# Folded projections in the first layer, another order for the first norm, and adaLN slabs moved by a table

## Chip, core and metric

One core of one Trainium2 chip runs the whole program once per call. The metric is the device time in microseconds (us) of that execution. Five instruction queues work side by side: TensorE (matmuls; PE in the rows, its weight loads PEld), VectorE (DVE), ScalarE (ACT), GpSimd (POOL) and SyncE (SP, which here only issues DMAs). Each queue runs its instructions in the order in which they were written; semaphores are the only coupling.

## What is computed

A batch of one sequence of 256 tokens and 1024 channels goes through three layers in float32. Layer 1 is a mixer (attention with a forget gate, beside a short convolution) and a SwiGLU network; layers 2 and 3 are attention (block-wise, then differential) and a SwiGLU network each, modulated by a vector `c`. Cut to what the change touches:

```python
def first_block(x, ...):
    h = rmsnorm(x, norm_mix_pre)
    proj = h @ w_in          # q, k, v, f_logit, g_b, g_c, hc, gate_conv, gate_attn
    ya = g_b * causal_depthwise_conv(g_c * hc, conv_w)
    yb = forgetting_attention(q, k, v, log_sigmoid(f_logit + b_f))
    merged = sigmoid(gate_conv) * (ya @ w_branch[0]) + sigmoid(gate_attn) * (yb @ w_branch[1])
    x = x + rmsnorm(merged @ w_out, norm_mix_post)
    return x + rmsnorm(swiglu(rmsnorm(x, norm_ffn_pre)), norm_ffn_post)

def second_block(x, c, ...):                  # twice
    mod = silu(c) @ ada_w[i] + ada_b[i]       # shift, scale, gain of two norms
    h = rms_norm(x, g0) * (1 + sc_a) + sh_a
    x = x + g_a * rms_norm(attention_i(h), g1)
    h = rms_norm(x, g2) * (1 + sc_f) + sh_f
    x = x + g_f * rms_norm(swiglu(h), g3)
```

## The kernel before

**Tiles.** The tokens are two tiles t of 128; a channel block k is 128 channels, so x is 2 x 8 blocks. Every weight comes as a slab of 128 x 2048 float32 (1 MB). 159 main slabs (`MAIN`: `v1` 0 and 1, `qk1` 2 to 5, `mix` 6 to 19, `branch` 20 to 23, `out1` 24 to 27, the first network from 28 on) and 48 `ada` slabs, which hold the rows of `ada_w`, form one stream. SyncE loads stream item i into `raw[i % 8]` (L500) once item i - 8 has left its place: a main slab when TensorE has used it, an `ada` slab when VectorE has summed it.

**Precision.** Each product is made of three TensorE products in a rounded format. ScalarE rounds a slab to `high` (L506, `act_round`), VectorE subtracts to `low` (L512, `dve_rest`, written over `raw`); activations are split the same way into `h_hi` and `h_lo`. `act_next` and `dve_next` round the slab three ahead of the one in work and, on VectorE, first sum the `ada` slabs that stand before it in the stream (L521, two reductions of 128 x 1024 for each slab). `load_order` holds the table `plan` that says behind which main slabs the `ada` slabs come.

**Two forms of a projection.** `pe_still` (L585 to L587) keeps weight blocks still and sends 256 tokens past: for each of 16 weight blocks high x hi, high x lo, low x hi, 48 matmuls of 256 columns into one PSUM bank. `pe_both` (L623, L628) sends hi and lo side by side: 16 matmuls of 512 columns for high, then 16 of 256 columns for low, into two banks; ScalarE copies the lo half out (`act_low`, L635) and VectorE adds the hi half (`dve_low`, L643 or L645; signal `joined`). Before, `pe_still` is used for the four `qk1`, for `mix` 0 to 5 and for gates 6 and 7 (12 slabs); everything later that could be folded is.

**Start.** x tile 0, x tile 1, slab 0 in two halves are loaded in this order. The sums of squares go half to ScalarE (L352), half to VectorE (L1486); GpSimd makes the power (L364); x is scaled (L369; of tile 1 the left half by GpSimd, L1686, the right half by ScalarE); TensorE transposes it (L320, `pe_turn`); ScalarE applies the column gain from PSUM into `work` (L332, `act_affine`); VectorE casts to `h_hi` (L346) and subtracts to `h_lo` (L348). `pe_first_values` starts the values product; the second `v1` slab follows in `pe_moving` (L668 to L670), and the gate logits are copied by VectorE (L1512) before TensorE adds them up (L1213).

**First norm behind a layer.** `branch` ends in `merged` (VectorE L1603, L1608, ScalarE L1409, VectorE L1611), `out1` is the wide product, and its post norm (`dve_post_norm`: L420, L358, L435, then L369) gives the scaled x that TensorE transposes in the middle of `out1`'s last products. On GpSimd, `pool_gain` stores a gain column (L486) and loads it as rows (L490).

## Time and profile before

| | us |
|---|---|
| median of 3 runs (lowest, highest) | 963.48 (962.64, 963.85) |
| profiled execution, its own time | 962.54 |
| its span, first to last instruction | 961.2 |
| TensorE busy | 953.2 |
| VectorE busy | 740.0 |
| ScalarE busy | 544.8 |

The span lies 1.3 us under the profiled execution's own time, and that execution 0.94 us under the median. Matmul ends are modelled and overlap, so the pitch of matmuls is read from start to start, and waits from the idle time in brackets behind a row.

### The profile page before, as it was taken

Reading aid. Unit: us, or ns where it says so; the run is one execution under the profiler, and the core shown is the slowest. Engines: PE = TensorE matmul, PEld = TensorE weight load, DVE = VectorE, ACT = ScalarE, POOL = GpSimd, SP = SyncE. Lnnn points to the kernel's source line nnn. Section 1 sums busy time; section 2 is a strip of 40 time slices with the busy share of each in tenths; the row PEclk is TensorE's granted clock in tenths of the full one; section 3 lists DMA queues with packets and bytes.
Section 4 is the critical chain, followed back from the end, with each engine's and each line's share of the span. In section 5 each row is a group of like instructions: output and inputs, shape, how many; then the busy total and the mean of one; then the engine's idle time right before and its main releaser. Section 6 shows DMA issues by size and latency. Waiting matters only on the chain.

```text
span 961.2 us, 13438 instructions
## 1 busy us (share of the span) xinstructions
PE 953.2 (99%) x5418; PEld 827.7 (86%) x5418; DVE 740.0 (77%) x1145; ACT 544.8 (57%) x838; POOL 34.2 (4%) x58
## 2 busy tenths in 40 slices
PE   9999999999999999999999999999999999999997
PEld 7999989888888888888888888888888888888886
DVE  7799978788877767988678878766897678766563
ACT  6745553565455656665565454656776675454551
POOL 2000000020000001000000000001000100000000
PEclk9999999999999999999999999999999999999999
DMA  9877788498777753776467677763743266668511
GB/s 366 335 276 263 262 308 313 173 200 343 269 295 300 286 204 135 270 269 264 185 248 296 247 293 271 270 250 137 241 138 125 88 243 239 219 184 320 176 44 45
DMA packets 33151, 225.64 MB, mean 235 GB/s; under 512 B 4058, under 2 KB 4341, under 8 KB 6720
## 3 DMA queue, kind: packets, MB, share of 16 engines
q1 hardware_dynamic: 30960, 219.43, 61.8%
q0 software_dynamic: 1696, 5.08, 2.0%
q8 instruction: 43, 0.70, 0.3%
q10 hardware_dynamic: 432, 0.26, 0.1%
q14 instruction: 20, 0.16, 0.0%
HBM read 223.49 MB, written 1.26 MB: 234 GB/s over the span
## 4 chain that ended last, share of the span: by engine, by line
PE 93%; DVE 2%; DMA 2%; ACT 2%; SPq 0%; POOL 0%; issue 0%; DVEq 0%
PE psum L623 30%; PE psum L628 16%; PE psum L668 10%; PE psum L669 10%; PE psum L670 10%; PE psum L585 3%; PE psum L586 3%; PE psum L587 3%; DMA raw<-in_qk 2%; PE psum L888 2%; PE psum L740 1%; PE psum L739 1%; PE psum L741 1%; PE psum L320 1%; PE psum L956 1%; PE psum L601 0%
## 5 line engine op out<-in xcount | busy, mean ns | idle before, releaser
L512 DVE TENSOR_TENSOR low<-raw,high 128x2048 fp32r<-128x2048 f32 (+1 forms) x160 | 361.1, 2275 | 95.1 <-ACT high L506 95.0
L506 ACT ACTIVATE high<-raw 128x2048 fp32r<-128x2048 f32 (+1 forms) x160 | 299.9, 1897 | 15.1 <-DMA raw<-in_moba_qk 4.8
L623 PE MATMUL psum<-h_both,high 128*128 128x512 f32 x1272 | 305.3, 392 | 0.0
L623 PEld LDWEIGHTS psum<-h_both,high 128*128 128x128 f32 x1272 | 235.5, 188 | 48.2 <-issue 1.5
L628 PEld LDWEIGHTS psum<-h_both,low 128*128 128x128 f32 x1312 | 168.3, 191 | 6.4
L628 PE MATMUL psum<-h_both,low 128*128 128x256 f32 x1312 | 170.2, 283 | 0.0
L668 PE MATMUL psum<-high,y_hi 128*128 128x512 f32 x328 | 129.3, 394 | 0.0
L669 PE MATMUL psum<-low,y_hi 128*128 128x512 f32 x328 | 128.1, 391 | 0.0
L670 PE MATMUL psum<-high,y_lo 128*128 128x512 f32 x328 | 127.8, 390 | 0.0
L635 ACT ACTIVATE work_v<-psum 128x256 f32<-128x256 f32 x120 | 45.6, 383 | 142.2 <-PE psum L628 142.2
L521 DVE CUSTOM_DVE_ANT_0 raw<-raw,c_row 128x1024 f32<-128x1024 f32 x96 | 113.4, 1219 | 0.0
L670 PEld LDWEIGHTS psum<-high,y_lo 128*128 128x128 f32 x328 | 61.6, 188 | 13.1
L668 PEld LDWEIGHTS psum<-high,y_hi 128*128 128x128 f32 x328 | 61.7, 188 | 11.9 <-DVE y_lo L978 0.2
L669 PEld LDWEIGHTS psum<-low,y_hi 128*128 128x128 f32 x328 | 61.8, 188 | 11.4
L643 DVE TENSOR_TENSOR work_v<-psum,work_v 128x256 f32<-128x256 f32 x120 | 47.9, 420 | 23.4 <-ACT work_v L635 23.3
L585 PE MATMUL psum<-h_both,high 128*128 128x256 f32 x192 | 55.3, 288 | 0.0
L586 PE MATMUL psum<-h_both,high 128*128 128x256 f32 x192 | 54.4, 283 | 0.0
L587 PE MATMUL psum<-h_both,low 128*128 128x256 f32 x192 | 54.4, 283 | 0.0
L809 ACT ACTIVATE y_hi<-work_v 128x512 fp32r<-128x512 f32 x30 | 19.0, 632 | 48.4 <-DVE work_v L831 48.4
L668 PE MATMUL psum<-high,h_both 128*128 128x512 f32 x104 | 41.6, 400 | 0.1
L670 PE MATMUL psum<-high,h_both 128*128 128x512 f32 x104 | 40.6, 391 | 0.0
L669 PE MATMUL psum<-low,h_both 128*128 128x512 f32 x104 | 40.6, 390 | 0.0
(195 smaller groups left out, 1033.6 us busy)
## 6 DMA issues: line engine op xcount, KB each, us to landing
raw<-in_gate_up SPq DMA_DIRECT2D x66, 1024.0 KB, 5.5
raw<-in_ada SPq DMA_DIRECT2D x48, 1024.0 KB, 4.9
raw<-in_down SPq DMA_DIRECT2D x33, 1024.0 KB, 4.9
raw<-in_mix SPq DMA_DIRECT2D x14, 1024.0 KB, 6.9
raw<-in_moba_qk SPq DMA_DIRECT2D x8, 1024.0 KB, 5.2
raw<-in_diff_qk SPq DMA_DIRECT2D x8, 1024.0 KB, 4.9
raw<-in_qk SPq DMA_DIRECT2D x4, 1024.0 KB, 16.2
raw<-in_branch SPq DMA_DIRECT2D x4, 1024.0 KB, 6.3
```

Source lines behind the costliest of these rows:

```text
L506: nc.scalar.activation(high[n % N_HI][:, s], raw[i % N_RAW][:, s], ACT.Copy).then_inc(*rounded.up(n if key is None else key))
L512: nc.vector.tensor_tensor(low[i % N_RAW][:, s], raw[i % N_RAW][:, s], high[n % N_HI][:, s].bitcast(F32), ALU.subtract).then_inc(*rest.up(key))
L521: last = nc.vector.tensor_tensor_reduce(out=w, in0=w, in1=c_row[:, :], scale=1.0, scalar=0.0, op0=ALU.mult, op1=ALU.add, accum_out=mod_raw ...
L585: nc.tensor.matmul(to, a, hi(k), start=first, stop=False)
L586: nc.tensor.matmul(to, a, lo(k), start=False, stop=False)
L587: m = nc.tensor.matmul(to, r, hi(k), start=False, stop=last and j > j0)
L623: nc.tensor.matmul(o[:, :], a, h_both[:, k, :, :], start=k == 0, stop=False)
L628: m = nc.tensor.matmul(o[:, 0:S], wl[:, k, j * P:(j + 1) * P], h_hi[:, k, :], start=False, stop=k == KC - 1)
L643: m = nc.vector.tensor_tensor(place[:, j, :], o, place[:, j, :], ALU.add)
L668: nc.tensor.matmul(psum[b][:, :], hi(k0 + k, t), vh, start=first, stop=False)
L669: nc.tensor.matmul(psum[b][:, :], hi(k0 + k, t), vl, start=False, stop=False)
L670: m = nc.tensor.matmul(psum[b][:, :], lo(k0 + k, t), vh, start=False, stop=last)
```

## The change

1. Twelve first-layer slabs go from `pe_still` to `pe_both`, with bank numbers fixed for some; `act_low` and `dve_low` take their results out, and the products that used to read PSUM now read the joined tile.
2. The first norm: `act_affine` writes `h_hi` itself, and `h_lo` is made block by block from PSUM with one `scalar_tensor_tensor`; tile 1 is scaled half by VectorE and half by ScalarE; slab 0's first half is loaded and rounded ahead of x's second tile; slab 1 is rounded in halves, and TensorE may begin on the first half; three filling matmuls go.
3. `plan`: 14, 11, 8, 11, 4 `ada` slabs in five stretches become 9, 14, 8, 13, 4. Before, 14 stood behind main slabs 4, 5, 6, 8, 9, 10, 12, 13, 15, 16, 17, 19, 20, 22; now 9 stand behind 9, 11, 13, 15, 18, 20, 22, 24, 27.
4. GpSimd waits for the scaled x of tile 1 before it stores a gain column (three places).

```diff
-    plan = [(14, 4, 22), (11, nets[0][0] + 4, nets[0][0] + 24), (8, nets[0][1] + 4, nets[1][0] - 2),
-            (11, nets[1][0] + 3, nets[1][0] + 26), (4, nets[2][0] + 4, nets[2][0] + 16)]
+    plan = [(9, 9, 27), (14, nets[0][0] + 2, nets[0][0] + 24), (8, nets[0][1] + 4, nets[1][0] - 2),
+            (13, nets[1][0] + 2, nets[1][0] + 25), (4, nets[2][0] + 4, nets[2][0] + 16)]
...
         def act_affine(stage, t, g):
-                o, to = psum[bank_of[stage, t, g]][:, (k - a) * P:(k - a + 1) * P], work_b[:, k, tile_of(t)]
+                o = psum[bank_of[stage, t, g]][:, (k - a) * P:(k - a + 1) * P]
+                to = (h_hi if stage == "in" else work_b)[:, k, tile_of(t)]
...
         def dve_split_h(stage, t, a, b):
+            if stage == "in":
+                ...
+                yield from dve.wait_ge(affined, (stage, t, k1 - 1))
+                for k in range(a, b):
+                    m = nc.vector.scalar_tensor_tensor(
+                        out=h_lo[:, k, w], in0=psum[bank_of[stage, t, g]][:, (k - k0) * P:(k - k0 + 1) * P], scalar=scale[:, k:k + 1],
+                        in1=h_hi[:, k, w].bitcast(F32), op0=ALU.mult, op1=ALU.subtract)
...
             def qk(g, keys):
-                yield from pe_still("qk1", 2 * keys + g, h_of, ready, [[(produced, ("k1", g)) if keys else (evacuated, ("q1", g))]])
+                yield from pe_both("qk1", 2 * keys + g, ready, at=(6, 7) if keys == 1 and g == 0 else (5, 6) if keys else (None, None))
...
-                yield from pe_still("mix", g, h_of, ready, [[(produced, ("conv", g))]])
+                yield from pe_both("mix", g, ready, at=(None, None) if g else (4, 6))
...
                 yield from dve_next("mix", 4 + g)
-                yield from dve.wait_ge(slab, ("mix", 4 + g))
-                yield from dve.wait_ge(evacuated, ("zc", g))
-                nc.vector.tensor_tensor(zc[:, two, :], pair(bank_of["mix", 4 + g, 0]), zc[:, two, :], ALU.mult).then_inc(
-                    *produced.up(("z", g)))
+                yield from dve_low(("mix", 4 + g), ya[:, two, :])
+                yield from dve.wait_ge(joined, ("mix", 4 + g, 1))
+                nc.vector.tensor_tensor(zc[:, two, :], ya[:, two, :], zc[:, two, :], ALU.mult).then_inc(*produced.up(("z", g)))
...
             yield from pool_post_norm(1)
+            yield from pool.wait_ge(scaled, (1, NT - 1, 1))
             yield from pool_gain(0, 1, 0)
...
         def sync():
-            for t in range(NT):
-                nc.sync.dma_start(x_res[:, t, :], dram["x"][tile_of(t), :]).then_inc(*x_in[t].up("rows", by=16))
             first, half = dram["v1"][0], SLAB // 2
+            nc.sync.dma_start(x_res[:, 0, :], dram["x"][tile_of(0), :]).then_inc(*x_in[0].up("rows", by=16))
             nc.sync.dma_start(raw[0][:, 0:half], first[:, 0:half]).then_inc(*raw_first.up("a", by=16))
+            nc.sync.dma_start(x_res[:, 1, :], dram["x"][tile_of(1), :]).then_inc(*x_in[1].up("rows", by=16))
             nc.sync.dma_start(raw[0][:, half:], first[:, half:]).then_inc(*raw_in[0].up(0, by=16))
```

The table of `ada` slabs moves instructions at places that the diff does not show. SyncE, the loads of the `out1` slabs (24 to 27), before:

```order
L500 DMA raw6<-in_out1 128x2048 [waits slab]
L500 DMA raw7<-in_out1 128x2048 [waits summed]
L500 DMA raw0<-in_out1 128x2048 [waits slab]
L500 DMA raw1<-in_out1 128x2048 [waits summed]
L500 DMA raw2<-in_gate_up1 128x2048 [waits slab]
```

and after, where `raw1` was held by slab 20, the first `branch` slab:

```order
L511 DMA raw7<-in_out1 128x2048 [waits summed]
L511 DMA raw0<-in_ada 128x2048 [waits slab]
L511 DMA raw1<-in_out1 128x2048 [waits slab]
L511 DMA raw2<-in_out1 128x2048 [waits summed]
L511 DMA raw3<-in_out1 128x2048 [waits slab]
L511 DMA raw4<-in_ada 128x2048 [waits slab]
```

Two `ada` slabs now stand among the `out1` slabs, and slab 25 waits for a slab that TensorE has used instead of one that VectorE has summed.

VectorE, between the first and the third `branch` slab (L1603 before and L1615 after are the products with the gates; `low6`, `low7` before are slabs 24 and 25), before:

```order
L1603 TENSOR_TENSOR work<-psum1,work 128x512 [waits slab]
L512 TENSOR_TENSOR low6<-raw6,high0 128x2048 [waits rounded]
L512 TENSOR_TENSOR low7<-raw7,high1 128x2048 [waits rounded]
L1603 TENSOR_TENSOR work<-psum2,work 128x512 [waits slab]
L1603 TENSOR_TENSOR work<-psum3,work 128x512 [waits slab]
L1603 TENSOR_TENSOR bias<-psum0,bias 128x512 [waits slab]
```

and after (`low7`, `low1` are slabs 24 and 25):

```order
L1615 TENSOR_TENSOR work<-psum1,work 128x512 [waits slab]
L523 TENSOR_TENSOR low7<-raw7,high0 128x2048 [waits rounded]
L532 ISA raw0,mod_raw<-raw0,c_row 128x1024 [waits raw_in0]
L532 ISA mod_raw 128x1
L532 ISA raw0,mod_raw<-raw0,c_row 128x1024
L532 ISA mod_raw 128x1
L486 SCALAR_TENSOR_TENSOR mod_raw<-mod_raw,mod_given 128x8 [waits summed]
L490 TENSOR_TENSOR mod_cols<-mod_raw,mod_given 128x8 [waits summed]
L523 TENSOR_TENSOR low1<-raw1,high1 128x2048 [waits rounded]
L1615 TENSOR_TENSOR work<-psum2,work 128x512 [waits slab]
L1615 TENSOR_TENSOR work<-psum3,work 128x512 [waits slab]
L1615 TENSOR_TENSOR bias<-psum0,bias 128x512 [waits slab]
```

A sum of an `ada` slab has come between slabs 24 and 25.

VectorE, ahead of the first post norm (L420 before, L431 after, is its first instruction), before:

```order
L1611 TENSOR_TENSOR h_both<-bias,h_both 128x2x256 [waits hi_made]
L512 TENSOR_TENSOR low1<-raw1,high3 128x2048 [waits rounded]
L512 TENSOR_TENSOR low2<-raw2,high4 128x2048 [waits rounded]
L512 TENSOR_TENSOR low3<-raw3,high5 128x2048 [waits rounded]
L420 TENSOR_TENSOR work<-psum4,gain0 128x512 [waits squared,gain_in0,produced]
```

and after:

```order
L1623 TENSOR_TENSOR h_both<-bias,h_both 128x2x256 [waits hi_made]
L523 TENSOR_TENSOR low3<-raw3,high3 128x2048 [waits rounded]
L532 ISA raw4,mod_raw<-raw4,c_row 128x1024 [waits raw_in4]
L532 ISA mod_raw 128x1
L532 ISA raw4,mod_raw<-raw4,c_row 128x1024
L532 ISA mod_raw 128x1
L523 TENSOR_TENSOR low5<-raw5,high4 128x2048 [waits rounded]
L523 TENSOR_TENSOR low6<-raw6,high5 128x2048 [waits rounded]
L431 TENSOR_TENSOR work<-psum4,gain0 128x512 [waits squared,gain_in0,produced]
```

One more sum stands among the three subtractions in front of the norm.

## Rows read from the trace of the kernel before

**Rows 1.** The page: parts 1 and 2, busy time and granted clock.

```profile
PE 953.2 (99%) x5418; PEld 827.7 (86%) x5418; DVE 740.0 (77%) x1145; ACT 544.8 (57%) x838; POOL 34.2 (4%) x58
PEclk9999999999999999999999999999999999999999
```

**Rows 2.** Waits of TensorE: who waited, for whom, us in all, times, longest.

```profile
PE psum L888 <- DVE ck L1552: 0.4, 1, 0.4
```

**Rows 3.** Timeline of TensorE (start us, us, line), then pieces of the chain.

```profile
26.21 0.28 PE L587 MATMUL psum<-h_both,low 128*128 128x256 f32 x1
...
31.96 0.28 PE L587 MATMUL psum<-h_both,low 128*128 128x256 f32 x1
```

```profile
119.06 1.91 PE psum L628 x16
120.97 3.65 PE psum L623 x16
```

**Rows 4.** Timeline of the first 25 us; last, VectorE's instructions grouped by shape.

```profile
4.87 0.63 ACT L352 ACTIVATE work_v<-x_res 128x512 f32<-128x512 f32 x1 [1.47 <-DMA x_res<-in_x]
...
6.30 0.63 ACT L352 ACTIVATE work_v<-x_res 128x512 f32<-128x512 f32 x1 [0.71 <-DMA x_res<-in_x]
...
16.86 6.70 DVE L512 TENSOR_TENSOR low<-raw,high 128x2048 fp32r<-128x2048 f32 x3 [0.25 <-ACT high L506]
...
19.21 0.19 PEld L668 LDWEIGHTS psum<-high,h_both 128*128 128x128 f32 x1 [0.66 <-DVE low L512]
...
23.47 0.67 DVE L1512 COPY work<-psum 16x512 f32<-16x512 f32 x1
...
24.89 0.38 PE L1213 MATMUL psum<-cols,work 16*128 16x8 f32 x2
...
L901 DVE SCALAR_TENSOR_TENSOR prob<-psum,c_q,const 128x128 f32<-128x128 f32 x8 | 2.8, 344 | 0.0
```

**Rows 5.** VectorE in the first layer: windows, two timeline rows, a group of the page.

```profile
34.00:100.00 66.00, 65.58 (x545) 62.93 (x544) 64.54 (x118) 34.25 (x59) 0.00 (x0) 1.00 0.73 271
...
38.32 1.22 DVE L521 CUSTOM_DVE_ANT_0 raw<-raw,c_row 128x1024 f32<-128x1024 f32 x1
...
44.13 0.86 DVE L1552 TENSOR_TENSOR ck<-psum,ck 8x256 fp32r<-8x256 f32 x2 [0.55 <-ACT ck L1364]
...
L643 DVE TENSOR_TENSOR work_v<-psum,work_v 128x256 f32<-128x256 f32 x120 | 47.9, 420 | 23.4 <-ACT work_v L635 23.3
```

The first row's columns are: stretch, its length, busy us of PE, PEld, DVE, ACT, POOL (instructions), granted clock, DMA share, GB/s.

**Rows 6.** Timeline of VectorE and GpSimd in the norms behind two networks.

```profile
378.62 1.19 DVE L369 TENSOR_SCALAR work<-x_res,stat 128x512 f32<-128x512 f32 x2 [0.66 <-POOL stat L364]
...
667.51 1.05 POOL L486 DMA_DIRECT2D gain_dram<-gain_col  x1
667.59 1.19 DVE L369 TENSOR_SCALAR work<-x_res,stat 128x512 f32<-128x512 f32 x2 [0.66 <-POOL stat L364]
```

**Rows 7.** Timeline from `branch` to the first post norm, four queues.

```profile
143.27 6.56 SPq L500 DMA_DIRECT2D raw<-in_out  x4
...
148.21 1.92 ACT L506 ACTIVATE high<-raw 128x2048 fp32r<-128x2048 f32 x1 [1.55 <-DMA raw<-in_out]
...
148.84 0.28 PE L585 MATMUL psum<-y_hi,high 128*128 128x256 f32 x1
...
152.61 2.29 DVE L512 TENSOR_TENSOR low<-raw,high 128x2048 fp32r<-128x2048 f32 x1 [0.16 <-ACT high L506]
...
157.68 0.69 DVE L1603 TENSOR_TENSOR bias<-psum,bias 128x512 f32<-128x512 f32 x1 [1.58 <-PE psum L587]
...
173.32 6.70 DVE L512 TENSOR_TENSOR low<-raw,high 128x2048 fp32r<-128x2048 f32 x3 [1.11 <-ACT high L506]
...
179.93 0.68 DVE L420 TENSOR_TENSOR work<-psum,gain 128x512 f32<-128x512 f32 x1
...
184.65 0.88 DVE L369 TENSOR_SCALAR work<-x_res,stat 128x512 f32<-128x512 f32 x2 [0.67 <-POOL stat L364]
...
185.28 1.06 PE L320 MATMUL psum<-const,work 128*128 128x128 f32 x8
```

More of the change, by code:

```diff
@@ L663, in pe_moving @@
                 for k in range(kcs):
+                    if n == 1 and k == kcs // 2:
+                        yield from pe.wait_ge(rest, n)
                     for signal, key in ready(k0 + k, t):
@@ L1171, in pe_first_values @@
                     nc.tensor.matmul(o[:, :], h_hi[:, k, tile_of(0)], wl[:, k, :], start=False, stop=False)
[L1172 to L1173 removed]
+                for k in ks:
+                    for signal, made in ready(k, 0):
+                        yield from pe.wait_ge(signal, made)
+                    nc.tensor.matmul(o[:, :], h_lo[:, k, tile_of(0)], wh[:, k, :], start=False, stop=False)
             o = yield from bank(("v1", 1, 0), *freed_by_values("v1")(1, 0), at=6)
```

134 lines of the change are left out of this document (68 added, 66 removed).

## Prediction

> **What bounds the kernel now.** I read the page's busy times first, then TensorE's waits, then the pitch of its matmuls, then the timelines of the places that the change touches. TensorE is busy 953.2 of 961.2 us, at a granted clock of 9 tenths or more in every slice [rows 1]; the only wait of it that the change aims at behind the start is one of 0.4 us, for `ck` from VectorE [rows 2]. So time can be saved in three ways only: fewer or cheaper matmuls, an earlier start, shorter waits; and anything that makes TensorE wait is paid in full. VectorE is the engine to watch. Between 34 and 100 us it is busy 64.5 of 66.0 [rows 5] and still makes TensorE wait hardly at all, because its work lies three slabs ahead. Where that lead ends, at the first post norm, the reader should look hardest: TensorE's transposes begin at 185.28, and the scaled x that they read comes from an instruction pair that begins at 184.65 [rows 7]; its first half ends some 0.5 later, so there is about 0.1 us to spare.
>
> **The folding.** A still slab is 48 matmuls: from 26.21 to 31.96, 48 starts on, is 5.75 us. A folded slab is 16 of 512 columns and 16 of 256: 3.65 + 1.91 = 5.56 [rows 3]. That is 0.19 a slab, for 12 slabs **-2.3** (-2.0 to -2.6, for first matmuls behind other work). What it adds lies on ScalarE (two copies, where there was one or none; it has idle time) and on VectorE: 24 additions of 256 columns from PSUM at 0.42 [rows 5], about 10 us. VectorE has no such room today, but the table takes 7 of 11 sums away that stood up to main slab 17; a sum is two reductions of 1.14 start to start (the row gives 1.22 with its tail), 2.3 together, so 16 us go. VectorE therefore gets lighter by some 6 us there.
>
> **The `ck` wait.** `ck` is ready once VectorE has worked off what is in front of it; the first tables' sums (two by then, 4.6 us) are gone and four additions (1.5) come. It should be ready near 43.1 in place of 45.0 [rows 5], while TensorE arrives about 1 us sooner than today. The wait goes: **-0.5** (0 to -0.6; the row says 0.4, start to start it is 0.58).
>
> **A new wait for banks.** Folded slabs take two banks, and these come free only when VectorE has added. The tight one is `mix` 0: its second bank is the second of `mix` 5, and only one pass of 16 matmuls and three transposes (2.2 us) lies between. In VectorE's queue, an `ada` sum (2.3), a subtraction (2.2) and two attention pieces stand ahead of that addition. Counted through its queue from `ck` on, I find it done some 0.3 late: **+0.3** (0 to +1.0).
>
> **The start.** x's second tile landed 1.43 us behind the first (4.87, 6.30); now half a slab of the same 512 KB goes between, so all that needs both tiles comes 1.4 later. The 16 new split instructions have a row like them: PSUM and SBUF in, 128 x 128, 0.344 each [rows 4], against pairs of a cast and a subtraction before. ScalarE's rounding of the first half fills the time that it waited. Followed through the four queues with these durations, VectorE comes to slab 1's subtraction at 17.0 (16.86 before) and to the copy of the logits at 23.7 (23.47). TensorE no longer waits 0.66 for all of slab 1, because a half is enough, is done with the values at 24.5, and starts the gate sums at about 24.6 in place of 24.89 [rows 4]: **-0.3** (-0.8 to +0.3). What is late next is VectorE's copy of the logits.
>
> **GpSimd's later stores.** In two norms the scaling pair takes 1.19, where it takes 0.88 elsewhere [rows 6, 7]; in one of them the store of the gain column, 1.05 long, begins 0.08 before it [rows 6]. TensorE stands waiting for that pair in both. Behind the new wait the store begins after it: twice 0.31, of which I take **-0.5** (0 to -0.6). Nothing on GpSimd behind the store is due for many us. The Trainium skill (SBUF — State Buffer, "Who interferes with whom") says that of VectorE in a two-port mode and GpSimd one blocks the other for a whole instruction. By that the stores could give back up to 1.05 each, 1.6 more than I take in all; the measured lengthening, 0.31, decides.
>
> **What the table adds.** Two `ada` slabs now stand among the `out1` slabs, and this is the costliest part.
> First, slab 25. Its load waits for the first `branch` slab, which TensorE leaves at 148.84; a load of this kind landed 4.94 after its issue (143.27 to 148.21), so it lands at 153.8. Rounding takes 1.92, to 155.7; the subtraction 2.2, to 158.0; two products with the gates 1.28, to 159.3. The third `branch` slab's product, which began at 157.68, is then 1.6 late. From there to 173.32 VectorE and ScalarE hand each other one step after the other, so the delay is not made up: the subtractions for `out1` begin at 174.9.
> Second, a sum of 2.3 us stands between them, in front of the norm. The norm's first instruction moves from 179.93 to 183.8, 3.9 later. I count no slack in the steps from there to the scaling, which follow on one another as before. So the scaled x is 3.9 late, and TensorE, with 0.1 to spare, stands for 3.8 [all rows 7]: **+3.8** (+2.2 if slab 25 lands in time, +4.0). TensorE has no other work to put there: what follows stands behind the transposes in its queue.
> The denser tables in the first two networks (14 for 11 and 13 for 11 sums) cost VectorE 7 and 5 us in stretches of some 150; at its mean of 77% [rows 1] it idles some 34 in such a stretch. They begin one and two slabs earlier, behind the norms' last steps. I cost them at **0** (0 to +0.5).
>
> **Sum.** -2.3 - 0.5 + 0.3 - 0.3 - 0.5 + 3.8 = +0.5 on the profiled execution's own 962.54, so 963.0. That execution lies 0.94 under the median of 963.48; moved by the same amount the median becomes **964.0**. A gain spread over the first layer is given back in one place. The bounds added up would be -2.4 to +3.8; they will not all fall on one side, so this case's own range is 961.9 to 966.2.
>
> **Rivals.**
> *No stall at the norm.* If VectorE reaches the norm in time after all (slab 25 earlier, the sum hidden in its waits for ScalarE, of which the last is 1.11 long [rows 7]), the rest stands: about -3.3, 960.2. For it: VectorE does idle on that stretch. Against: the queue is in order, and the sum is written behind the first of the three subtractions, after all these waits.
> *TensorE's clock falls in the stall* (slower than before). The trace shows 1.00 everywhere, but behind the start there is no TensorE gap near 3.8 us in it, so it cannot tell. At the lower of the two levels (1.2 instead of 2.4 GHz) a 512-column matmul would take twice its 0.228 (3.65 over 16). The 12 matmuls right behind the transposes would cost 2.7, the next 24 another 5.5; I take 4, so 968.0. It decides from the length of the gap: with the sum alone, at 2.2, I would not expect it. The Trainium skill (TensorE: Matmul & The Clock Gate, "Why this matters for your kernels") warns of idle gaps between bursts for this reason; no run here shows one.
> *Banks wait on VectorE.* If its lead in the folded stretch is shorter than I counted, the wait at `mix` 0 repeats at other pairs: with 1 us at three places 2 to 3 more, 966.5. For it: 98% busy before. Against: 6 us less work there now.
>
> **How the numbers follow.** Forecast 0.60, no stall 0.22, clock 0.10, banks 0.08. A measurement of this kernel tells a change of about 0.2% (1.9 us) from none, so same means 961.6 to 965.4. Of the forecast 0.05 lies below, 0.07 above; no stall gives faster 0.22; clock gives slower 0.10; banks slower 0.05 and same 0.03. Faster 0.27, same 0.51, slower 0.22. The range takes in the forecast's bounds and the no-stall case, and leaves the clock case and the ends: 960.0 to 966.4.
>
> **What would show it.** In the profile after: folded slabs at 5.56 in the first layer; TensorE at its first attention scores without a wait for `ck`; the scaling pair back at 0.88 in the later norms; in the norm behind `out1` a TensorE gap of 2 to 4 us before the transposes, released by VectorE's scaling, with an `ada` sum between the subtractions ahead of it. Wrong would be: no gap there (then faster), a granted clock under 1 behind it, or waits of TensorE on `joined` between 45 and 110.

## The result, and the profile after

The changed kernel takes 967.39 us (median of 6 runs, 967.03 to 967.81); the kernel before took 962.87 (6 runs beside them). The ratio is 1.0046, with an interval of 1.0033 to 1.0059: slower by 4.5 us, where 964.0 was predicted with a range of 960.0 to 966.4. The profiled execution has a span of 966.1 against 961.2.

The waits of TensorE (engine and line, for whom, us in all, times, longest) tell most of it. The wait for `ck` [rows 2] is gone; behind the start three others are new, and they carry 5.8 us.

```profile
PE psum L321 <- DVE work L380: 3.3, 1, 3.3
PE psum L681 <- DVE y_lo L848: 1.5, 1, 1.5
PE psum L681 <- DVE low L523: 1.0, 1, 1.0
```

Lines have moved: L321 are the transposes (L320 before), L380 the scaling (L369), L523 the subtraction of a slab's high part (L512), L532 an `ada` sum (L521), L681 the moving matmuls (L668), L654 the addition of a folded slab (L643), L848 the low half of the hidden rows (L835).

The timeline of TensorE at its landmarks: the gate sums, a folded slab, the first scores, the first `branch` slab, the transposes behind `out1`, those of the second tile, and those at the end of the first network.

```profile
24.99 0.38 PE L1218 MATMUL psum<-cols,work 16*128 16x8 f32 x2
...
31.65 3.82 PE L634 MATMUL psum<-h_both,high 128*128 128x512 f32 x16
35.30 2.07 PE L639 MATMUL psum<-h_both,low 128*128 128x256 f32 x16
37.21 0.73 PE L1232 MATMUL psum<-gate_f,const 128*128 128x8 f32 x6
...
44.20 0.49 PE L901 MATMUL psum<-work 64*128 64x128 f32 x2
...
140.58 0.28 PE L596 MATMUL psum<-y_hi,high 128*128 128x256 f32 x1
...
187.49 1.88 PE L321 MATMUL psum<-const,work 128*128 128x128 f32 x8 [3.30 <-DVE work L380]
...
198.33 1.06 PE L321 MATMUL psum<-const,work 128*128 128x128 f32 x8
...
375.67 1.06 PE L321 MATMUL psum<-const,work 128*128 128x128 f32 x8
```

A folded slab takes 37.21 - 31.65 = 5.56, as costed. The first scores begin without a wait. TensorE comes to `branch` at 140.58; before it came at 143.07, so 2.5 us are won by there. Then it loses them and more. The same landmarks before, beside the transposes at 185.28 [rows 7]:

```profile
143.07 0.28 PE L585 MATMUL psum<-y_hi,high 128*128 128x256 f32 x1
...
194.47 1.06 PE L320 MATMUL psum<-const,work 128*128 128x128 f32 x8
...
369.98 1.06 PE L320 MATMUL psum<-const,work 128*128 128x128 f32 x8
```

In four stages, from the starts of the same transposes in both timelines:

| stage, us | before | after | difference |
|---|---|---|---|
| to the transposes behind `out1` | 185.28 | 187.49 | +2.2 |
| from there to those of the second tile | 9.19 | 10.84 | +1.65 |
| from there to the end of the first network | 175.51 | 177.34 | +1.83 |
| from there to the end of the span | 591.2 | 590.4 | -0.8 |

The first line is 2.5 won and 4.7 lost: 1.2 at the last `out1` slab and 3.45 ahead of the transposes (start to start, less the matmul's own pitch). The timelines of VectorE and, in the first row, of ScalarE show what was late.

```profile
151.38 1.92 ACT L517 ACTIVATE high<-raw 128x2048 fp32r<-128x2048 f32 x1 [3.40 <-DMA raw<-in_out]
...
151.82 1.22 DVE L532 CUSTOM_DVE_ANT_0 raw<-raw,c_row 128x1024 f32<-128x1024 f32 x1
...
154.51 2.29 DVE L523 TENSOR_TENSOR low<-raw,high 128x2048 fp32r<-128x2048 f32 x1
...
157.91 0.68 DVE L1615 TENSOR_TENSOR bias<-psum,bias 128x512 f32<-128x512 f32 x1
...
173.39 2.29 DVE L523 TENSOR_TENSOR low<-raw,high 128x2048 fp32r<-128x2048 f32 x1 [1.11 <-ACT high L517]
175.60 1.22 DVE L532 CUSTOM_DVE_ANT_0 raw<-raw,c_row 128x1024 f32<-128x1024 f32 x1
...
182.29 0.69 DVE L431 TENSOR_TENSOR work<-psum,gain 128x512 f32<-128x512 f32 x1
...
186.86 0.88 DVE L380 TENSOR_SCALAR work<-x_res,stat 128x512 f32<-128x512 f32 x2 [0.66 <-POOL stat L375]
```

The sum behind slab 24 (151.82) stands ahead of slab 25's subtraction, and the third `branch` product comes at 157.91, where it came at 157.68 [rows 7] though TensorE is 2.5 ahead. Slab 25's load is not what held the subtraction last: it had landed by 151.38, its rounding was done at 153.30, and VectorE came out of the sum at 154.51. The sum behind slab 27 (175.60) stands between the last subtractions, and the norm begins at 182.29 in place of 179.93. So VectorE reaches slab 27's subtraction when it did before (173.39 and 173.32), TensorE's 2.5 us of gain are waited away, and the sum adds 2.3.

The second line of the table is the clock. Windows of 1 us (stretch, length, busy us of PE, PEld, DVE, ACT, POOL with instructions, granted clock, DMA share, GB/s):

```profile
184.00:185.00 1.00, 0.20 (x1) 0.00 (x0) 1.00 (x2) 0.46 (x1) 0.00 (x0) 1.00 0.00 0
...
187.00:188.00 1.00, 0.51 (x3) 0.54 (x4) 1.00 (x3) 0.00 (x0) 0.00 (x0) 0.79 0.98 418
...
189.00:190.00 1.00, 1.00 (x4) 0.84 (x3) 0.75 (x3) 1.00 (x5) 0.00 (x0) 0.50 1.06 451
190.00:191.00 1.00, 1.00 (x4) 0.78 (x3) 0.84 (x3) 0.73 (x3) 0.00 (x0) 0.51 0.70 295
191.00:192.00 1.00, 1.00 (x6) 0.81 (x5) 0.88 (x2) 0.00 (x0) 0.00 (x0) 1.00 0.00 0
```

TensorE did nothing from 184.2 to 187.5; when it goes on, the granted clock is at half its level (1.2 in place of 2.4 GHz) until 191. The eight transposes take 1.88, where they took 1.06 [rows 7]. The page's strip of 40 slices shows 9 throughout, as before: a fall of some 3.4 us doesn't show in slices of 24 us.

The third line is the wait for `y_lo` at the end of the first network, where the prediction had put 0. VectorE, ScalarE and TensorE there:

```profile
356.61 2.29 DVE L523 TENSOR_TENSOR low<-raw,high 128x2048 fp32r<-128x2048 f32 x1 [1.11 <-ACT high L517]
358.82 0.75 DVE L654 TENSOR_TENSOR work_v<-psum,work_v 128x256 f32<-128x256 f32 x2
...
359.60 0.63 ACT L814 ACTIVATE work_v<-work_v 128x512 f32<-128x512 f32 x1 [2.48 <-DVE work_v L654]
360.14 1.90 ACT L517 ACTIVATE high<-raw 128x2048 fp32r<-128x2048 f32 x1
...
362.07 2.29 DVE L523 TENSOR_TENSOR low<-raw,high 128x2048 fp32r<-128x2048 f32 x1 [2.50 <-ACT high L517]
...
366.45 0.69 DVE L848 TENSOR_TENSOR y_lo<-work_v,y_hi 128x512 fp32r<-128x512 f32 x1 [0.70 <-ACT y_hi L822]
...
367.29 0.47 PE L681 MATMUL psum<-high,y_hi 128*128 128x512 f32 x1 [1.49 <-DVE y_lo L848]
```

Read it as a ring: VectorE's addition (358.82) releases ScalarE's silu (359.60), behind which ScalarE rounds the next slab (360.14), which releases VectorE's next subtraction (362.07), behind which stands its next addition. In this turn VectorE idles 2.50 and ScalarE 2.48, each waiting for the other, so neither idle time lets the two catch up. From one low half of the hidden rows to the next, three slabs on, the ring takes 16.05 where no sum stands in it (338.75 to 354.80 in VectorE's timeline); TensorE takes 16.57 for three slabs (322.99 to 339.56 before). Two groups of the page (busy, mean ns, idle before and who ended it) show how much of the engines' idle time such waits are: 103.7 of VectorE's 223 us, and 79.7 of ScalarE's 424:

```profile
L523 DVE TENSOR_TENSOR low<-raw,high 128x2048 fp32r<-128x2048 f32 (+1 forms) x161 | 361.4, 2262 | 103.7 <-ACT high L517 103.6
...
L814 ACT ACTIVATE work_v<-work_v 128x512 f32<-128x512 f32 x30 | 19.0, 632 | 79.7 <-DVE work_v L654 79.7
```

The small gain in the last line of the table is in part the later store. The two scaling pairs of [rows 6] are back at 0.88:

```profile
384.31 0.88 DVE L380 TENSOR_SCALAR work<-x_res,stat 128x512 f32<-128x512 f32 x2 [0.66 <-POOL stat L375]
...
672.70 0.88 DVE L380 TENSOR_SCALAR work<-x_res,stat 128x512 f32<-128x512 f32 x2 [0.66 <-POOL stat L375]
```

### The profile page after: what moved, and what is told of

The parts are those of the page before. It is cut to its first block, busy times and chain, and to the rows that moved or that the text cites. A ratio compares the mean times of both kernels' runs of the same rounds, so it can differ in the third digit from the quotient of the medians.

```text
span 966.1 us, 13085 instructions
## 1 busy us (share of the span) xinstructions
PE 953.3 (99%) x5220; PEld 819.1 (85%) x5220; DVE 743.2 (77%) x1169; ACT 542.0 (56%) x859; POOL 32.3 (3%) x57
## 4 chain that ended last, share of the span: by engine, by line
PE 80%; DVE 14%; ACT 5%; issue 1%; POOL 0%; DVEq 0%; ACTq 0%
PE psum L634 27%; PE psum L639 15%; PE psum L681 9%; PE psum L682 9%; PE psum L683 9%; DVE low L523 7%; ACT high L517 3%; DVE raw L532 2%; PE psum L901 1%; PE psum L321 1%; PE psum L753 1%; PE psum L752 1%; PE psum L754 1%; PE psum L1196 1%; DVE bias L654 1%
## 5 line engine op out<-in xcount | busy, mean ns | idle before, releaser
L523 DVE TENSOR_TENSOR low<-raw,high 128x2048 fp32r<-128x2048 f32 (+1 forms) x161 | 361.4, 2262 | 103.7 <-ACT high L517 103.6
L634 PE MATMUL psum<-h_both,high 128*128 128x512 f32 x1464 | 352.0, 392 | 0.0
L634 PEld LDWEIGHTS psum<-h_both,high 128*128 128x128 f32 x1464 | 270.5, 188 | 56.2 <-issue 2.4
L639 PEld LDWEIGHTS psum<-h_both,low 128*128 128x128 f32 x1504 | 192.8, 191 | 7.3
L639 PE MATMUL psum<-h_both,low 128*128 128x256 f32 x1504 | 195.1, 283 | 0.0
L681 PE MATMUL psum<-high,y_hi 128*128 128x512 f32 x328 | 129.3, 394 | 1.5 <-DVE y_lo L848 1.5
L532 DVE CUSTOM_DVE_ANT_0 raw<-raw,c_row 128x1024 f32<-128x1024 f32 x96 | 113.4, 1219 | 0.0
L646 ACT ACTIVATE work_v<-psum 128x256 f32<-128x256 f32 x120 | 42.4, 376 | 77.2 <-PE psum L639 77.2
L681 PEld LDWEIGHTS psum<-high,y_hi 128*128 128x128 f32 x328 | 61.7, 188 | 13.8 <-issue 1.9
L814 ACT ACTIVATE work_v<-work_v 128x512 f32<-128x512 f32 x30 | 19.0, 632 | 79.7 <-DVE work_v L654 79.7
L654 DVE TENSOR_TENSOR work_v<-psum,work_v 128x256 f32<-128x256 f32 x120 | 46.5, 418 | 16.1 <-ACT work_v L646 16.0
L681 PE MATMUL psum<-high,h_both 128*128 128x512 f32 x104 | 42.2, 405 | 1.0 <-DVE low L523 1.0
L848 DVE TENSOR_TENSOR y_lo<-work_v,y_hi 128x512 fp32r<-128x512 f32 x30 | 20.8, 692 | 20.9 <-ACT y_hi L822 20.9
L375 POOL TENSOR_TENSOR stat<-stat,minus_half 128x1 f32<-128x1 f32 x24 | 13.3, 552 | 687.0 <-DVE stat L369 687.0
```

The source lines that it names most:

```text
L523: nc.vector.tensor_tensor(low[i % N_RAW][:, s], raw[i % N_RAW][:, s], high[n % N_HI][:, s].bitcast(F32), ALU.subtract).then_inc(*rest.up(key))
L532: last = nc.vector.tensor_tensor_reduce(out=w, in0=w, in1=c_row[:, :], scale=1.0, scalar=0.0, op0=ALU.mult, op1=ALU.add, accum_out=mod_raw ...
L634: nc.tensor.matmul(o[:, :], a, h_both[:, k, :, :], start=k == 0, stop=False)
L639: m = nc.tensor.matmul(o[:, 0:S], wl[:, k, j * P:(j + 1) * P], h_hi[:, k, :], start=False, stop=k == KC - 1)
L646: nc.scalar.activation(place[:, j, :], psum[bank_of[*key, j]][:, S:2 * S], ACT.Copy, scale=scale).then_inc(*evacuated.up(("low", *key, j)))
L654: m = nc.vector.tensor_tensor(place[:, j, :], o, place[:, j, :], ALU.add)
```

## The experiments

All ratios are to the kernel before on the same chip. The first theory: the table of `ada` slabs makes all three losses, and the rest of the change is a gain. The rivals: folding and the new first norm make them, or VectorE is simply full.

| run | edit | us | ratio, interval |
|---|---|---|---|
| e1 | changed kernel, table of before | 966.73 | 1.0034 (1.0022 to 1.0047) |
| e2 | kernel before, changed table | 966.64 | 1.0036 (1.0023 to 1.0049) |
| e3 | first nine sums end at slab 22 | 964.09 | 1.0006 (0.9997 to 1.0015) |
| e4 | 12 sums in the first layer, 11 in the first network | 964.63 | 1.0015 (1.0006 to 1.0024) |
| e5 | nine sums behind 14 to 22, 11 in the network, 3 in the second attention | 968.30 | 1.0053 (1.0040 to 1.0066) |
| e6 | the network's part of e5 alone | 972.75 | 1.0099 (1.0085 to 1.0113) |
| e7 | matmuls put into the gap | 965.53 | 1.0024 (1.0014 to 1.0034) |
| e8 | e5 without the folding | 970.89 | 1.0083 (1.0069 to 1.0096) |
| e9 | nine behind 14 to 22, 14 early in the network | 965.21 | 1.0020 (1.0011 to 1.0028) |
| e10 | 6, 16, 8, 14, 4 sums | 964.74 | 1.0009 (1.0001 to 1.0018) |
| e11 | slab 27's sum moved forward | 963.63 | 0.9998 (0.9989 to 1.0006) |
| e12 | slab 24's sum moved forward | 964.85 | 1.0008 (0.9997 to 1.0019) |
| e13 | 9, 13, 8, 14, 4 sums | 961.79 | 0.9978 (0.9969 to 0.9987) |
| e14 | 10, 12, 8, 14, 4 sums | 961.64 | 0.9977 (0.9967 to 0.9987) |
| e15 | kernel before, table of e14 | 966.57 | 1.0037 (1.0024 to 1.0050) |
| e16 | e14 again, beside e15 | 962.23 | 0.9986 (0.9977 to 0.9995) |

The table's line in the code, `plan`, holds for each stretch the number of sums and the first and last slab behind which they stand. The networks begin at slabs 28, 77 and 126, and `nets[0][0]` is 28; the second network's 14 sums in e10 and e13, which their expectations put behind slabs 70 to 92, stand behind 79 to 101. In the diffs below the entries that are the same are left out.

### The table alone, and all but the table

```
 e1: changed kernel with
-    plan = [(9, 9, 27), (14, nets[0][0] + 2, nets[0][0] + 24), ..., (13, ...), ...]
+    plan = [(14, 4, 22), (11, nets[0][0] + 4, nets[0][0] + 24), ..., (11, ...), ...]
 e2: kernel before with the opposite edit
```

> The changed kernel with the table of ada slabs of the kernel before (14 sums from slab 4 to 22, 11 in the first network, 11 in the second); all else as changed. Theory 'the table pays for the folding': the stall before the transposes of the norm behind out1 (3.45), the clock fall behind it (about 1.6), the wait at the last out1 slab (1.2) and the wait at the end of the first network (1.65) all go, 7.9 in all; but VectorE, which was 64.5 of 66.0 us busy between 34 and 100 us, gets the folding's 24 additions (10 us) with nothing taken away, so TensorE waits for joined sums, 4 to 8 us in all: 963.5 to 967.5, with no stall at the norm. Rival 'the folding costs nothing on VectorE': no waits on joined sums, 959.5. Rival 'folding and first norm make the stalls': the gap at the norm is there as in the changed kernel, 967 or more.

> The kernel before with the changed table of ada slabs alone (9 sums from slab 9 to 27, 14 in the first network, 13 in the second). Theory 'the table makes the stalls': the same places are late as in the changed kernel, the last out1 slab (0 to 1.2), the norm behind out1 (3 to 4, with granted clock near 0.5 behind it, 1.6 more), the end of the first network (1.65); the wait for ck goes (-0.5). Sum +5 to +8: 968 to 971. Rival 'folding and first norm make the stalls': no gap over 1 us at the norm, 962 to 963.

Each half of the change alone costs 3.2 to 3.3 us. e2, the table alone, has the same gap at the norm, 3.29, and the same half clock behind it, so the first norm and the folding don't make it. The wait for `ck` is gone there too. It came out below its 968 to 971: the wait at the network's end is 0.6 there, and there is none at `out1`.

e1, the rest alone, loses in another place. The wait for `ck` is back, at 1.1, so it was the table that took it away. TensorE waits for a folded slab's addition in the attention stretch, as the first theory had it, and there too the clock falls. At the norm, where no gap was expected, one of 1.16 stays though no sum stands among the `out1` slabs. Its timeline and its windows:

```profile
84.63 3.41 PE L634 MATMUL psum<-h_both,high 128*128 128x512 f32 x8 [2.58 <-DVE bias L654]
```

```profile
84.00:85.00 1.00, 0.37 (x1) 0.37 (x2) 0.97 (x3) 0.00 (x0) 0.00 (x0) 0.53 1.05 442
85.00:86.00 1.00, 1.00 (x3) 0.79 (x3) 0.97 (x4) 0.66 (x2) 0.00 (x0) 0.50 1.02 434
```

VectorE is busy 0.97 of each of these us: it is full there, and the folding's additions need the room that the thinner table makes. So the two halves belong together; the fault is where the table put what it took away.

### Which of the two sums makes the gap

```
 e3:  (9, 9, 27) -> (9, 9, 22)
 e11: sums behind 9, 11, 13, 15, 17, 18, 20, 22 and 24   (27's moved to 17)
 e12: sums behind 9, 11, 13, 15, 17, 18, 20, 22 and 27   (24's moved to 17)
```

> The changed kernel with the first nine sums of the table spread from slab 9 to 22 in place of 9 to 27, so that no ada slab stands among the out1 slabs. Theory: the wait at the last out1 slab (1.2), the gap at the norm behind out1 (3.45) and the clock fall (1.6) go, the wait of 1.65 at the end of the first network stays: 967.4 - 6.2 = 961.2. Rival 'the two are one lateness' (the wait at the network's end comes from the norm's stall): that goes too, 959.5. Rival 'VectorE is merely full': nine sums in a shorter stretch make TensorE wait on joined sums between 60 and 120 us, 1 to 3 us, 962.5 to 964.

> The changed kernel with the ada slab behind slab 27 moved forward to slab 17; the one behind slab 24 stays. Theory: without the sum between the last subtractions the gap at the norm is 1.2 to 2.2, the granted clock stays at 1.00 behind it, the wait at the last out1 slab (0 to 1.2) stays, the network's end keeps its 1.65: 964 to 966. Rival 'slab 24's ada makes the whole lateness': gap of 3 or more with the clock at half, 967.

> The changed kernel with the ada slab behind slab 24 moved forward to slab 17; the one behind slab 27 stays. Theory: the sum of 2.3 between the last subtractions comes on top of the 1.2 that other tables show: gap 3 to 3.6, clock at half behind it (1.6), the network's end keeps its 1.65: 966 to 967.4. Rival 'it takes both': gap under 2, no clock fall, 964 to 965.

The row of the transposes behind `out1` in e3, then in e11 (with the last `out1` slab ahead of it) and in e12:

```profile
185.82 1.06 PE L321 MATMUL psum<-const,work 128*128 128x128 f32 x8 [1.02 <-DVE work L380]
```

```profile
176.23 0.50 PE L681 MATMUL psum<-high,h_both 128*128 128x512 f32 x1 [1.29 <-DVE low L523]
...
185.69 1.07 PE L321 MATMUL psum<-const,work 128*128 128x128 f32 x8 [0.99 <-DVE work L380]
```

```profile
185.64 1.94 PE L321 MATMUL psum<-const,work 128*128 128x128 f32 x8 [2.87 <-DVE work L380]
```

Slab 27's sum lengthens the gap by its own length: e11 differs from the changed kernel only in that this sum has moved to slab 17, and the gap is 1.15 in place of 3.45 (start to start, as all that follow): 2.3. Slab 24's sum is the second part. Without it (e12) the wait at the last `out1` slab is gone, and the gap is 3.03, that is 0.75 without slab 27's 2.3; with it the wait and the rest of the gap are 1.2 + 1.15 = 2.35 in the changed kernel. So slab 24's sum makes 1.6 and 0.75 are neither's: 2.3 + 1.6 + 0.75 = 4.65. This takes both moved sums to cost nothing behind slab 17, which was not shown; in e11 the wait at the last `out1` slab is 1.45, a little longer. e12 came out below its 966 to 967.4; the last section comes back to it. e3 came out at 964.09 in place of 961.2: a gap of 1.17 was left, and a wait of 1.0 for ScalarE stands at 113; that five sums up to slab 15 made it is likely and was not tried.

A gap of 1.12 to 1.18 was left at the norm in e3, e5, e9 to e11, e13 and e14, and in e1 and e15. It is VectorE's lateness against TensorE, brought along from ahead of the third `branch` product. Before, VectorE waited 1.58 for TensorE there [rows 7], 14.61 behind TensorE's first `branch` matmul; no other trace shows a wait of VectorE there. It comes 15.55 behind that matmul in e12, 16.25 in e10, 16.69 in e5 and 17.33 in the changed kernel. From there the steps are a fixed chain: from VectorE's subtraction of slab 27 to the transposes it is 11.8 us in e3 (174.01 to 185.82), 11.8 in e5 (172.56 to 184.38) and 12.0 before (173.32 to 185.28 [rows 7]). A small lateness shows as the gap at the norm alone (0.35 in e4, where it is 15.15). A longer one makes TensorE wait at the last `out1` slab too, and the gap stays at 1.15. The folding is not needed for it: e15 and e8, without the folded slabs, have the gap of 1.18 and 1.17 as well. Sums behind slabs 20 to 22 that hold buffers, the theory of e10, are not it either: without them the gap is still 1.12. Which step ahead of `branch` makes VectorE late was not tried.

### What the clock costs

```
+                for _ in range(26 if (stage, t, g) == (0, 0, 0) else 0):
+                    nc.tensor.matmul(o[:, 0:S], y_hi[:, 0, 0:P], y_hi[:, 0, :], start=True, stop=True)
                 for k in range(a, b):
```

> The changed kernel with 26 matmuls of 256 columns (3.1 us at 0.12 each) put on TensorE ahead of the transposes of the norm behind out1, that is into its gap of 3.45; they write a bank that the transposes then overwrite. Theory: the gap's length stays, but the granted clock stays at 1.00 behind it, and the transposes and matmuls behind it run at full pitch: 967.4 - 1.6 = 965.8. Rival 'the slow pitch behind the gap is something else than the clock, or the work is paid for anyway': 967.4 or, if the added matmuls lengthen the gap, up to 970.

965.53 against 967.39: 1.86 less (2.1 by the ratios), for 3 us of work whose result nobody reads. In the timeline the added matmuls fill the gap and the transposes come no earlier than the gap's end; in the windows the clock stays at its higher level where it had been at half.

```profile
183.95 3.27 PE L315 MATMUL psum<-y_hi 128*128 128x256 f32 x26
187.28 1.12 PE L323 MATMUL psum<-const,work 128*128 128x128 f32 x8
```

```profile
189.00:190.00 1.00, 1.00 (x6) 0.84 (x5) 0.96 (x3) 1.00 (x5) 0.00 (x0) 1.00 1.01 426
```

So the price of the fall is a cost of its own, beside the gap's.

### The end of the first network

```
 e4:  (9, 9, 27), (14, 28 + 2, 28 + 24)  ->  (12, 6, 22), (11, 28 + 4, 28 + 24)
 e6:  first stretch as changed; (11, 28 + 4, 28 + 24); 3 sums behind 114, 118, 122
 e9:  (9, 14, 22), (14, 28 + 2, 28 + 16)
 e10: (6, 14, 19), (16, 28 + 2, 28 + 19), ..., (14, 77 + 2, 77 + 24)
 e13: (9, 13, 21), (13, 28 + 2, 28 + 24), ..., (14, 77 + 2, 77 + 24)
 e14: (10, 13, 22), (12, 28 + 3, 28 + 24), ..., (14, 77 + 2, 77 + 24)
```

> The changed kernel with 12 sums from slab 6 to 22 and 11 in the first network (the network's part of the table as before), the rest of the table as changed. Theory: no stall at the norm, and none at the end of the first network, since that comes from 14 sums in place of 11: 967.4 - 6.2 - 1.65 = 959.5, less what three more sums cost in the first layer (7 us of VectorE's work; 0 to 2 us): 959.5 to 961.5. Rival 'the network's end is late from the folding or the later stores, not from its density': the wait of 1.5 stays there, 961.2 or more.

> The changed kernel with 11 sums in place of 14 in the first network (from slab 32 to 52, as before) and the three left over among the second attention's slabs; the nine first sums stay at 9 to 27, two of them among out1. Theory: the wait at the end of the first network (1.65) goes and nothing else: 965.7, with the gap of 3.45 at the norm and the clock fall still there. Rival 'that wait is what the norm's stall leaves behind': it stays, 967.4.

> The changed kernel with its counts of sums (9, 14, 8, 13, 4) at other slabs: the nine one behind each of the slabs 14 to 22, the 14 of the first network one behind nearly each of the slabs 30 to 44 in place of 30 to 52. Theory: at the end of the first network VectorE is late because the last sums come too close to it; a stretch of 8 slabs without sums lets the exchange with ScalarE catch up (0.5 for each three slabs), so the wait of 1.65 goes though the count is the same. Norm behind out1 as in e5_late_dense (gap 1.2, clock at 1.00): 961 to 962. Rival 'the count of 14 decides': the wait stays, 962.5 to 964.

> As e9_net_early, but with six sums in the first layer (behind slabs 14 to 19), 16 in the first network (slabs 30 to 49) and 14 in the second (slabs 70 to 92). Theory: the gap of 1.2 that is left at the norm behind out1 comes from the raw buffers: sums behind slabs 20 to 22 hold buffers, so the out1 slabs land late; without them VectorE's steps ahead of the norm begin 1 to 2 us earlier and the gap goes: 959.5 to 961. Rival 'the gap is the length of the norm's own steps': it stays at 1.2, 961 to 962; or the denser networks make waits of 1 to 3 at their ends, 962 to 965.

> The changed kernel with another table alone: nine sums behind the slabs 13 to 21, 13 in the first network (slabs 30 to 52) and 14 in the second (70 to 92). Theory: with 14 sums the hidden rows' low halves of the first network come 8.7 us late (against the kernel before) by their fourth piece and still 3.3 late at the last, and TensorE waits for what is over some 1.7 of that; the second network with 14 ended 1.4 late and with 13 0.3, without a wait. So 13 in the first network ends under 1.7 late and the wait goes; at the norm behind out1 a gap of 1.2 stays and the clock stays at 1.00: the transposes there near 184.2, 960 to 961.5 in all. Rival 'the first network is late from its first two sums, not from the count': a wait of 1 or more stays, 961.5 to 963.

> As e13_13_14 with ten sums behind the slabs 13 to 22, 12 in the first network (from slab 31) and 14 in the second. Theory: the network ends less than 1 us late, no wait; in the first layer VectorE has one more sum (2.3) in its waits for ScalarE, which holds one raw buffer longer: the transposes at the norm 0 to 1 later than in e13_13_14: 960 to 962. Rival as there: a wait of 1 or more at the network's end.

The measure is when VectorE begins the last low half of the hidden rows, counted from the transposes of the network's first norm (second tile). Rows: before, after, and e13.

```profile
359.24 0.69 DVE L835 TENSOR_TENSOR y_lo<-work_v,y_hi 128x512 fp32r<-128x512 f32 x1 [0.70 <-ACT y_hi L809]
```

```profile
277.38 0.69 DVE L848 TENSOR_TENSOR y_lo<-work_v,y_hi 128x512 fp32r<-128x512 f32 x1 [0.70 <-ACT y_hi L822]
```

```profile
358.76 0.69 DVE L848 TENSOR_TENSOR y_lo<-work_v,y_hi 128x512 fp32r<-128x512 f32 x1 [0.70 <-ACT y_hi L822]
```

The first is the last piece before: 359.24 - 194.47 = 164.8. In the changed kernel it is 366.45 - 198.33 = 168.1. The second row is the changed kernel's fourth piece, 277.38 - 198.33 = 79.0, where the kernel before had 70.3. So VectorE was 8.7 us late at the fourth piece, and six pieces and 89 us later it has made up 5.4 of it.

| sums in the network | run | last piece | TensorE's wait |
|---|---|---|---|
| 11 | before, first network | 164.8 | 0 |
| 14 | after, first network | 168.1 | 1.5 |
| 14 | e2, first network | 167.2 | 0.6 |
| 16, dense early | e10, first network | 168.9 | 1.6 |
| 13 | after, second network | 165.1 | 0 |
| 14 | e10, second network | 166.2 | 0 |
| 13 | e13, first network | 165.3 | 0 |
| 12 | e14, first network | 164.8 | 0 |

What the stage loses is what the lateness has over some 1.5 us: 1.83 for 3.3 in the changed kernel, 0.90 for 2.4 in e2, 2.63 for 4.1 in e10, where the named wait is only 1.6 of it. It came with the table and didn't depend on the stall ahead of it (e3 and e11 have it, without the long gap; e4 and e6, with 11 sums, have none, the latter with the long gap). e9 refuted putting the sums early to leave time at the end: VectorE got so late in the middle that TensorE waited four times between 233 and 266, 3.9 us in all, and the stage took 179.84 in place of 175.51; it came out at 965.21, above both what was expected and its rival. Why 14 sums leave 3.3 in the first network and 1.4 in the second was not tried.

e4 shows the other wall: 964.63 where 959.5 to 961.5 was expected. It took the network's wait away, but three more sums in the first layer brought e1's wait back in the attention stretch (3.1, and the clock behind it). e10, with six sums in the first layer, has the earliest transposes behind `out1` (183.87) and loses that in the network again. e13 and e14 came out at 961.8, which is 0.3 above what was expected, and 961.6, which is within it; both are some 0.2% faster than the kernel before. The wait went with 13 sums that begin at the same slab, so the count, with the closer spacing that it brings, made it.

### Three sums in the second attention

```
 e5: (9, 14, 22), (11, 28 + 4, 28 + 24), ..., (3, 110 + 4, 110 + 12), ...
```

> The changed kernel with another table alone: the nine first sums one behind each main slab from 14 to 22 (behind the attention stretch, none among out1), 11 sums in the first network as in the kernel before, and the three that are left over among the second attention's slabs. Theory: with the sums at 9 to 22 VectorE came out of the attention stretch 2.8 us late and never made it up, since from there it and ScalarE only hand slabs to each other with a period as long as TensorE's; 2.5 us of waiting in each such step take one sum (2.3) without lengthening it. So the gap of 1.2 at the norm goes as well as the waits at out1, the clock fall and the wait at the network's end: 958.5 to 960. Rival 'one sum a slab doesn't fit': VectorE gets later with each slab, a gap of 1 to 3 at the norm, 961 to 964. Rival 'three sums in the second attention stall it': 1 to 2 more there.

It took 968.30 where 958.5 to 960 was expected. Up to the second attention it had no wait at the network's end and full clock at the norm, though the gap of 1.2 stayed there; the transposes behind `out1` began at 184.38. Then one sum of 2.3 us, with two short instructions behind it, made TensorE wait 4.6. e6 has the same wait, and so came out at 972.75 in place of 965.7, though the wait it was to take away is gone. VectorE's sum, then TensorE's timeline and a window behind it:

```profile
716.54 1.22 DVE L532 CUSTOM_DVE_ANT_0 raw<-raw,c_row 128x1024 f32<-128x1024 f32 x1
```

```profile
723.82 0.79 PE L1112 MATMUL psum<-work_v,work 128*128 128x128 f32 x2 [4.56 <-DVE work L656]
```

```profile
727.00:728.00 1.00, 1.00 (x4) 0.81 (x3) 0.94 (x4) 1.00 (x1) 0.00 (x0) 0.50 0.00 0
```

From the norm's transposes ahead of this attention to those behind it, it takes 784.11 - 667.55 = 116.6 against 777.81 - 668.22 = 109.6 before: 7.0 us for sums that VectorE had room for on the mean, of which 4.6 are the wait and most of the rest the clock, at half until 729.

### What the folding is worth

```
 e8:  e5 with pe_still in place of pe_both in qk1 and mix, and the evacuations of before
 e15: kernel before with the table of e14
 e16: e14
```

> As e5_late_dense, but with the folding of the first layer undone (its 12 slabs of qk1 and mix as 48 matmuls of 256 columns, as in the kernel before; the start, the later stores and the new table stay). Theory: 12 times 0.19 = 2.3 us more than e5_late_dense (2.0 to 3.0, with the 24 additions gone from VectorE): 961 to 962.5. Rival 'the folding is given back in waits': within 0.5 of e5_late_dense.

> The kernel before with the table of e14_10_12 alone; no folding, the old start and the old stores. Theory 'the folding earns it': this table makes no stall at out1 or at a network's end, and without the folding TensorE reaches the norm behind out1 some 2 us later than in e14_10_12, so the gap of 1.2 there is smaller; the wait for ck (0.5) goes, since no sum stands in front of it: 962 to 963.5, that is 0.5 to 2 us over e14_10_12. Rival 'the table earns it': the same time as e14_10_12 within 0.3.

> e14_10_12 once more, so that it stands beside e15_before_e14 on the same chip: 0.9977 of the kernel before, as it was (0.9967 to 0.9987).

Unfolded, e5 takes 970.89 in place of 968.30: 2.6 more, where 12 slabs of 0.19 were 2.3; in the two traces TensorE comes to `branch` 2.2 apart (142.62 and 140.40). And on one chip the table of e14 takes 966.57 without the rest of the change and 962.23 with it, 4.3 apart, where 0.5 to 2 was expected (e14's ratio repeats as 0.9986, less than the first time but below 1 with its whole interval). So the rival that the table earns the gain falls: by itself it costs. It is more than the folding's 2.6. In the traces of e15 and e16, whose spans are 4.0 apart, 2.3 are won by `branch` (143.16 and 140.83), 1.1 is a wait for ScalarE at 424 that only e15 has, and 0.35 the later store at 672.

## Why the prediction was wrong

Step by step, in its own order.

**Folding: -2.3.** Right. 5.56 a slab in the timeline, 2.6 in e8.

**The `ck` wait: -0.5.** Right; no wait at 44.20. `ck` is ready at 42.3; the terms given (45.0 less 4.6 and 1.5 more) make 41.9, not the 43.1 that was written.

**A new wait for banks: +0.3.** It didn't come: TensorE has no wait on a joined slab in the first layer. The same mechanism, with VectorE fuller, is what e1 and e4 show at 2.6 and 3.1.

**The start: -0.3.** Not shown. In fifteen traces with the new start the gate sums begin between 24.75 and 25.07, 24.90 on the mean; in the three with the old one at 24.89, 24.52 and 25.44, 24.95 on the mean. In the changed kernel VectorE's copy of the logits begins at 24.10 where 23.7 was forecast, and a wait of TensorE for `wf_both` (0.5, at 17.57) is new.

**GpSimd's later stores: -0.5.** Half right. Both pairs are at 0.88, but only the second had held TensorE up: from 483.09 to 668.22 it was 185.13, and 184.76 after, 0.37 less, 0.35 of it between the last two transposes (9.63 and 9.28; e2 and e15, with the old stores, 9.62 and 9.63). In the norm at 379 TensorE's transposes follow its last matmul by as much before as after.

**The table at the norm: +3.8.** The place is right, and slab 27's sum cost the 2.3 that was put for it. The other half, 1.6 for slab 25, has its size by luck: slab 24's sum made 1.6, but as an instruction in VectorE's queue, not by the late load that was forecast, which landed at 151.38 in place of 153.8 and was not waited for last. The load was counted from 148.84, a time of the kernel before, though the prediction had TensorE 2.8 earlier by then. The 0.75 that neither sum makes had no term: the sum adds TensorE's gain up to `branch` and the stall behind it in full, which holds only if VectorE, the two delays aside, comes 2.8 earlier as well; it did not. In all the stall measures 4.65.

**The denser tables: 0 (0 to +0.5).** This step failed. It measures +1.83 in the first network. The argument was that at a mean of 77% VectorE idles 34 us in such a stretch, which would take 7 more. But much of that idle time is waiting in a ring with ScalarE, 2.5 us at a time. A sum that just fits into one wait costs nothing: from 140.75 to 146.22 VectorE goes from one subtraction to the next in 5.47 with a sum between them, and in e10 from 136.68 to 142.13 in 5.45 with none. That what goes beyond makes both engines late is argued from the ring; what is measured is 8.7 us of lateness, of which 5.4 were made up in 89. The shares on the page could not tell this; the column that says what ended the idle time before a group of instructions could have, and VectorE's timeline of before at the end of the network has the same 2.50 ahead of its subtractions.

**The rival on the clock: 0.10, +4.** It came about. The gap was foreseen at 3.8, and the prediction had set 2.2 as too short, so with 3.8 forecast its chance should not have been 0.10 beside 0.60 for that forecast. The price of 4 was too high: 1.65 in the trace and 1.86 by e7. It had been worked out for 12 matmuls and half of 24 more; the clock was back after 3.4 us, in which TensorE had done the eight transposes (0.8 more) and four matmuls (0.2 more each). The Trainium skill (TensorE: Matmul & The Clock Gate, "Why this matters for your kernels") warns of gaps between bursts; the trace agrees, with 0.50 behind a gap of 3.3.

Together: -2.5 up to `branch`, +4.65, +1.65, +1.83 and -0.8 make +4.8, against +0.5 predicted. Of the 4.3 between them the network is 1.8, the clock 1.65 and the norm 0.85. The range's upper end left the clock case out and had only 0.5 for the networks; the bounds of the terms themselves, +3.8 in all, reach 967.3, but the prediction set its range narrower, because they would not all fall on one side.

## What to carry to other kernels

An engine's idle share is room for new work only if its waits end on nobody who waits for it in turn; look in the profile at what ended the idle time, and where two engines end each other's, count a ring with a period, not a share. Background work may be as long as one wait in the ring and must not stand in the few steps that lead to the engine that bounds the kernel: one sum of 2.3 us in front of the norm cost 2.3 and the clock, one too many in a network 1.8. When a change frees time in one stage by moving work, cost the stage that receives it as closely as the one that is freed; here the same change with another table runs at 0.998 to 0.999 of the kernel before in place of 1.0046.

## What the runs showed of the hardware

TensorE's granted clock fell at gaps of 2.58 (e1), 2.87 (e12), 3.1 (e4), 3.3 (after, e2, e6) and 4.6 us (e5), and it stayed at 1.00 behind the waits of 1.0 to 1.2 at the norm (e1, e3, e5, e8 to e10). It need not be at half when TensorE goes on: in e6 the eight transposes behind a gap of 3.31 take 1.06, at full pitch, and the stage is still 1.6 longer.

```profile
187.28 1.06 PE L321 MATMUL psum<-const,work 128*128 128x128 f32 x8 [3.31 <-DVE work L380]
```

How long it stays is not the same either: some 3.4 us in the changed kernel and in e1, some 6.8 in e5 and in e12. In e1, e5 and e12 it fell before the gap had ended. In e12, with a gap of 2.9, it seems not to be the same from one execution to the next: twelve of them take 963.38 to 966.95, with a mean granted clock from 1.000 in the shortest to 0.995 in the longest, which is the profiled one.

```profile
185.00:186.00 1.00, 0.36 (x2) 0.39 (x3) 0.99 (x3) 0.00 (x0) 0.00 (x0) 0.50 1.03 434
...
190.00:191.00 1.00, 1.00 (x4) 0.81 (x3) 0.13 (x1) 0.00 (x0) 0.00 (x0) 0.50 0.00 0
191.00:192.00 1.00, 1.00 (x4) 0.76 (x4) 0.00 (x0) 0.00 (x0) 0.00 (x0) 0.63 0.00 0
```

From the norm's transposes to those of the second tile it takes 197.69 - 185.64 = 12.05 there, 2.9 more than the 9.19 of the kernel before. The other spans of e12 are 962.1 to 962.9 with a mean clock of 0.999 or 1.000 and 963.3 to 964.1 with 0.997 or 0.998. That the same gap can cost nothing, some 1.3 or some 3 us by the clock alone would fit this, but only the longest execution has a trace.
